# A two-block network on one core: the layer norms' mean from DVE's addition, routing reordered, constant products in PE's waits

## The chip, the core and the metric

The kernel is one program on one of the eight cores of a Trainium2 chip. The core's engines have instruction streams of their own and meet through semaphores: TensorE (PE, matrix products), VectorE (DVE), ScalarE (ACT), GpSimd (POOL) and SyncE (SP, which here issues the transfers from device memory). The metric is device microseconds for one execution. PE's clock has two levels, 1.2 and 2.4 GHz; the profile gives the granted clock of a stretch as a share of the higher one (PEclk).

## What is computed

The input is 256 tokens of 1024 features, f32. First block, two layers of this form (all f32, 2816 hidden columns in the feed-forward parts):

```
h = h + 0.5 * rmsnorm(swiglu(rmsnorm(h, g1), w_gate, w_up, w_down), g2)
h = h + rmsnorm(mixer(rmsnorm(h, g3)), g4)
h = h + 0.5 * rmsnorm(swiglu(rmsnorm(h, g5), w_gate, w_up, w_down), g6)

def mixer(u):                       # u @ w_in, split in z, xbc, dt, u5, g_a, g_b
    y_a = ssd_branch(z, xbc, dt) @ w_branch_a     # conv, silu, chunked state space, group norm
    y_b = s5_branch(u5) @ w_branch_b              # complex diagonal scan, gelu, glu
    return (sigmoid(g_a) * y_a + sigmoid(g_b) * y_b) @ w_out
```

Second block, two layers, `ALPHA = (2 * DEPTH) ** 0.25`:

```
layer 0: main = short convolution mixer;  ffn = swiglu (dense)
layer 1: main = causal attention of 12 heads with rotary positions;  ffn = 8 experts, 2 for each token
x = layer_norm(ALPHA * x + concat(main, memory_attention) @ w_o)
x = layer_norm(ALPHA * x + ffn)

def layer_norm(x, g, b):            # mean and variance over the 1024 features
    mu = mean(x);  var = mean((x - mu) ** 2)
    return (x - mu) * rsqrt(var + 1e-5) * g + b
```

## The kernel before

Every large product is made of three: weights and activations are each split into a high part (f32 rounded to the matrix format) and a low part, and hi x hi, lo x hi and hi x lo are added up in PSUM. A weight chunk is 128 x 2048 f32 (1.05 MB). SP loads it into one of three slots of `raw`; ACT rounds it into `w_hi` (`convert`, L1157) once PE has used the slot's last chunk; DVE subtracts (`w_lo`, L1594) and signals `weights_ready`; PE multiplies. Each engine's order is written out by hand, and all engines walk the same list of chunks. Loops on the chip run over the two layers of the first block (PE only), the steps of a feed-forward part (three chunks a step) and the experts.

PSUM has eight banks. Banks 0 to 3 hold the accumulated output of a part, by token or by feature; banks 4 to 7 take the columns of the current chunk, which ACT evicts.

Stage borders. When a part's output stands in PSUM, ACT squares and sums it, takes the root (L1169), DVE inverts it, scales and adds to `H` (L1640), and for the next part's norm the same is done with `H`; DVE writes `scaled` (a view of `G`, L1617). PE waits for `scaled_ready` in `turn_stream` (L674), transposes 16 tiles of 128x128 into banks 0 to 3, ACT makes `x_hi` out of each pair of tiles, DVE `x_lo`, and PE's first product (L612) follows. In the second block the border is `layer_norm`: DVE adds `ALPHA * H` and the part's output for each half of the tokens (L2067), ACT sums each half with a copy into a spare tile (L1425), DVE forms minus the mean (L2071, event `centered`), ACT squares with that bias and sums (L1173), root, inverse, and DVE writes `H` (L2077, `h_ready`), which PE turns (L674).

Inside the first block's mixer, the state-space branch ends with a norm over four groups of features: ACT squares a group (L1374, `group_sq`), PE sums over features with a matrix of ones (`sum_features`, L686, f32 products of 128x256), ACT takes the root (L1323), DVE inverts and stages (`k_hi`, `k_lo`), and PE multiplies with `w_branch_a`. The output projection (`token_chunk(C_OUT + i, i, 4)`, L665) waits for the merge of both branches on DVE (L1952).

Attention goes over pairs of heads: PE scores (L927), DVE maximum, ACT exponent and sum, DVE division (L2106), PE turns the probabilities (L936), ACT copies them, PE multiplies with the values (L947).

The experts. PE computes 16 logits columns (L1016), DVE picks the two best experts (`masks_ready`), PE counts ranks (`ranks`), DVE makes `slot_of` and the number of passes (`n_pass`, event `routed`; one pass if no expert has more than 128 tokens). In a pass DVE writes `pick` (L2220), PE gathers the expert's tokens out of `H` (L1036), ACT and DVE make `x_hi` and `x_lo` (`expert_inputs`, L1514 and L2244), and then 88 steps follow (8 experts, 11 steps): `front` and `back` (two halves of the contraction, L1059), the hidden tile's turn (L1073), and `down` (L1084 to L1086). The weights have a ring of three buffers for each of front, back and down, converted by ACT (`high`, L1526) and DVE (`low`, L2250). SP loads the first front and back early, and the rest after `routed`. Before, ACT and DVE convert `down` 0 ahead of `expert_inputs`:

```
            with n.loop(act, passes, "pass"):
                high("down", 0)
                expert_inputs()
                high("front", 1)
                silu()
```

Of the kernel before, what the change touches and what calls it, by code (L numbers as in the profile page):

```python
# [27 lines left out]
P = 128  # L28
T = 256
D = 1024  # L30
# [202 lines left out]
def build(nc, a, out):  # L233

    ctx = ExitStack()
    with ctx:
# [48 lines left out]
        def flat(tiles):  # L285
# [74 lines left out]
                 "gains_in prm_psum prm_ready setup_done h_ready squared rooted xf_ready xh_ready x_ready gain_in weighed scaled_ready turned logit_ready "  # L360
# [7 lines left out]
                 "picked gathered scattered scatter_turned scatter_ready hidden_ready hidden_turned kh_ready y_copied sum_added mean_sum "  # L368
# [235 lines left out]
        def _(pe):  # L604
# [4 lines left out]

            def product(dst, slot, hi, lo, w0, start):  # L610

                mm(dst, w_hi[:, slot, w0:w0 + P], hi, start=start, stop=False, skip_group_check=True)  # L612
                mm(dst, w_lo[:, slot, w0:w0 + P], hi, start=False, stop=False, skip_group_check=True)  # L613
                return mm(dst, w_hi[:, slot, w0:w0 + P], lo, start=False, stop=True, skip_group_check=True)  # L614
# [208 lines left out]
            def mixer():  # L823
# [17 lines left out]
                ssd_output(7)  # L841
                end_run()
# [20 lines left out]
                n.due("acc_read")  # L863
                zero_acc(4)
# [8 lines left out]
            with n.loop(pe, DEPTH, "layer"):  # L873
                pe.wait_ge(s["gains_in"], n.due("gains_in", 16 * 10))
                for i in range(2):
                    last = nc.tensor.transpose(PS[:, 7, 96 * i:96 * i + 96], prm_rows[0:96, i, :], cst("ident", 96, 0, 96))
                last.then_inc(s["prm_psum"], n.one("prm_psum"))
                pe.wait_ge(s["prm_ready"], n.due("prm_ready"))
                turn_stream(scaled, "scaled_ready")
                ffn(rows=True)  # L880
                turn_stream(scaled, "scaled_ready")
                mixer()
                turn_stream(scaled, "scaled_ready")
                ffn()
# [33 lines left out]
            def attention(heads):  # L918
# [34 lines left out]
                for p in range(pairs):  # L953
                    if p:
                        outputs(p - 1)
                    if p + 2 < pairs:
                        scores(p + 2)
                    turn(p)
# [21 lines left out]
            attention(heads_a)  # L980
            zero_acc()
            for i in range(4):
                token_chunk(B_WO1 + i, i)
            turn_stream(H, "h_ready")
            ffn()
            turn_stream(H, "h_ready")
# [17 lines left out]
            end_run(waiting=True)  # L1004
            swap(rope_at[10])
            pe.wait_ge(s["roped"], n.due("roped", 2))
            attention(heads_b)
            zero_acc()
            for i in range(4):
                token_chunk(B_WO2 + i, i)  # L1010
            turn_stream(H, "h_ready")
# [6 lines left out]
            last.then_inc(s["logits"], n.one("logits"))  # L1018
            pe.wait_ge(s["masks_ready"], n.due("masks_ready"))
# [6 lines left out]
            last.then_inc(s["ranks"], n.one("ranks"))  # L1026
            pe.wait_ge(s["routed"], n.due("routed"))
# [93 lines left out]
            with n.loop(pe, passes, "pass"):  # L1121
                pe.wait_ge(s["sum_added"], n.due("sum_added"))
                gather(turned=False)
                zero_sum()
                pe.wait_ge(s["x_ready"], n.due("x_ready", 2))
# [13 lines left out]
                turn_hidden(wait=True)  # L1139
                down()  # L1140
# [4 lines left out]
        def _(act):  # L1145
# [275 lines left out]
            def layer_norm(split=True, late=None):  # L1421
                near_root()
                for t in range(2):
                    act.wait_ge(s["xf_ready"], n.due("xf_ready"))
                    last = fn(unused_2[:, t, :], H[:, t, :], ACT.Copy, accum_out=sums[:, 0, t:t + 1])  # L1425
                last.then_inc(s["mean_sum"], n.one("mean_sum"))
                act.wait_ge(s["centered"], n.due("centered"))
                for t in range(2):
# [78 lines left out]
            fn(rsm[:, 5, :], rsm[:, 4, :], ACT.Exp).then_inc(s["route_exp"], n.one("route_exp"))  # L1507
            act.wait_ge(s["routed"], n.due("routed"))
# [48 lines left out]
            with n.loop(act, passes, "pass"):  # L1557
                high("down", 0)
                expert_inputs()
# [19 lines left out]
        def _(dve):  # L1579
# [484 lines left out]
            def layer_norm(src, split=True, late=None):  # L2064

                for t in range(2):
                    stt(H[:, t, :], H[:, t, :], ALPHA, src[:, t, :], MULT, ADD).then_inc(s["xf_ready"], n.one("xf_ready"))  # L2067
                dve.wait_ge(s["xf_ready"], n.last("xf_ready"))
                dve.wait_ge(s["gain_in"], n.due("gain_in", 32))
                dve.wait_ge(s["mean_sum"], n.due("mean_sum"))  # L2070
                then_on(ts(sums[:, 2, :], sums[:, 0, :], -1.0 / D, None, MULT), "centered")  # L2071
# [106 lines left out]

            def small(i):
# [12 lines left out]

            dve.wait_ge(s["logits"], n.due("logits"))
# [17 lines left out]
            v.memset(moe_sum[:, :, :], 0.0)  # L2211
# [5 lines left out]

            def gather_pick():
                for t in range(2):
                    ins = ts(pick[:, t, :], cst("iota", P, 0, P), cur[:, t:t + 1], None, EQ)  # L2220
                return ins

            def first_pick():

                then(v.tensor_copy(cur[:, 0:2, None], slot_of[:, :, 0:1]))
                gather_pick().then_inc(s["picked"], n.one("picked"))
# [70 lines left out]
            with n.loop(dve, passes, "pass"):  # L2297
                first_pick()
                low("down", 0)
                expert_inputs()  # L2300
# [22 lines left out]
                then(ts(slot_of, slot_of, -float(SLOTS), None, ADD))  # L2323
            layer_norm(moe_sum, split=False)
# [52 lines left out]
```

## Time and profile before

| what | value |
|---|---|
| median of 3 runs | 3215.32 us (3211.72 to 3215.64) |
| profiled execution | 3210.52 us |
| its span, first to last instruction | 3208.7 us |
| mean granted clock of PE | 0.955 |
| PE busy | 2953.6 us, 92% of the span |
| DVE busy | 2233.0 us, 70% |
| ACT busy | 1673.4 us, 52% |
| GpSimd busy | 74.2 us, 2% |
| read from device memory | 616.81 MB, 193 GB/s over the span |

The engines run side by side, so their shares don't add up to 100%. A busy PE is not always a fast one: where the granted clock is 0.5, the same product is busy for nearly twice as long. In a list of waits an engine's idle time stands beside the instruction that ended it and the one that released it.

### The profile page before, as it was taken

How to read it: one execution, taken by the hardware profiler on the slowest of the kernel's cores; microseconds unless marked ns; L12 is line 12 of the kernel's file. 1: busy time of each engine (PE TensorE's matmuls, PEld its weight loads, DVE VectorE, ACT ScalarE, POOL GpSimd, SP SyncE). 2: the span in 40 equal slices, each digit the busy share in tenths (PEclk: the TensorE clock that was granted, in tenths of full speed). 3: DMA queues.
4: the chain of work that ended last, by engine and by line, in shares of the span. 5: the costliest groups of instructions: out<-in, count | busy, mean ns of one | idle time of the engine just before them, and what ended most of it. 6: DMA issues, size and time to landing. Idle time of an engine off the chain costs nothing.

```text
span 3208.7 us, 51731 instructions
## 1 busy us (share of the span) xinstructions
PE 2953.6 (92%) x20597; PEld 2645.5 (82%) x20597; DVE 2233.0 (70%) x2614; ACT 1673.4 (52%) x1838; POOL 74.2 (2%) x68
## 2 busy tenths in 40 slices
PE   8988899989989988898989998998679999999997
PEld 7988898979989888888879896998467877787775
DVE  5778975655556779857555554555658888888887
ACT  4444566334444444563344443444446776677665
POOL 0000013000000000030000000000000000000000
PEclk9998999999999988999999998999879999999999
DMA  7553342446545533433545453555079999999995
GB/s 238 167 155 105 93 139 86 158 143 199 177 156 185 177 105 94 119 118 108 176 156 196 159 183 118 178 176 171 14 262 328 344 336 342 328 327 343 351 327 191
DMA packets 488733, 619.87 MB, mean 193 GB/s; under 512 B 34689, under 2 KB 439059, under 8 KB 488595
## 3 DMA queue, kind: packets, MB, share of 16 engines
q1 hardware_dynamic: 488595, 617.91, 58.3%
q8 instruction: 101, 1.65, 0.2%
q14 instruction: 37, 0.30, 0.0%
HBM read 616.81 MB, written 1.05 MB: 193 GB/s over the span
## 4 chain that ended last, share of the span: by engine, by line
PE 77%; DVE 14%; ACT 5%; issue 3%; DMA 0%; DVEq 0%; SPq 0%; ACTq 0%
PE PS L1059 13%; PE PS L612 12%; PE PS L613 12%; PE PS L614 12%; PE PS L665 12%; DVE w_lo L1594 3%; PE PS L1084 3%; PE PS L1086 3%; PE PS L1085 3%; ACT w_hi L1157 2%; ACT w_hi L1526 1%; PE PS L1094 1%; PE PS L794 1%; PE PS L1036 1%; PE PS L756 1%
## 5 line engine op out<-in xcount | busy, mean ns | idle before, releaser
L612 PE MATMUL PS<-x_hi,w_hi 128*128 128x256 f32 x3360 | 976.4, 291 | 11.5 <-DVE x_lo L2061 7.1
L613 PE MATMUL PS<-x_hi,w_lo 128*128 128x256 f32 x3360 | 966.8, 288 | 0.0
L614 PE MATMUL PS<-x_lo,w_hi 128*128 128x256 f32 x3360 | 965.5, 287 | 0.0
L1594 DVE TENSOR_TENSOR w_lo<-raw,w_hi 128x2048 fp32r<-128x2048 f32 x313 | 711.6, 2288 | 330.7 <-ACT w_hi L1157 330.0
L1157 ACT ACTIVATE w_hi<-raw 128x2048 fp32r<-128x2048 f32 x313 | 598.6, 1913 | 397.4 <-PE PS L665 248.0
L612 PEld LDWEIGHTS PS<-x_hi,w_hi 128*128 128x128 f32 x3360 | 662.1, 197 | 23.3 <-issue 12.0
L613 PEld LDWEIGHTS PS<-x_hi,w_lo 128*128 128x128 f32 x3360 | 662.4, 197 | 1.9
L614 PEld LDWEIGHTS PS<-x_lo,w_hi 128*128 128x128 f32 x3360 | 661.3, 197 | 0.0
L1059 PE MATMUL PS<-w_hi,x_hi 128*128 128x512 f32 x704 | 285.3, 405 | 9.5 <-DVE x_lo L2244 6.7
L1059 PE MATMUL PS<-w_lo,x_hi 128*128 128x512 f32 x704 | 276.7, 393 | 0.0
L1059 PE MATMUL PS<-w_hi,x_lo 128*128 128x512 f32 x704 | 275.3, 391 | 0.0
L2250 DVE TENSOR_TENSOR w_lo<-raw,w_hi 128x2048 fp32r<-128x2048 f32 x96 | 219.7, 2288 | 40.2 <-ACT w_hi L1526 39.8
L1659 DVE TENSOR_TENSOR k_hi<-act_out,PS 128x256 fp32r<-128x256 f32 x110 | 46.3, 420 | 279.4 <-PE PS L614 277.6
L2250 DVE TENSOR_TENSOR w_lo<-XC,w_hi 128x2048 fp32r<-128x2048 f32 x88 | 201.7, 2292 | 41.6 <-ACT w_hi L1526 41.4
L665 PE MATMUL PS<-w_hi,k_hi 128*128 128x512 f32 x568 | 179.9, 398 | 15.2 <-DVE k_lo L1952 13.6
L1526 ACT ACTIVATE w_hi<-raw 128x2048 fp32r<-128x2048 f32 x96 | 183.8, 1915 | 14.0 <-PE PS L1086 14.0
L665 PE MATMUL PS<-w_lo,k_hi 128*128 128x512 f32 x568 | 177.6, 394 | 0.0
L665 PE MATMUL PS<-w_hi,k_lo 128*128 128x512 f32 x568 | 177.1, 393 | 0.0
L1526 ACT ACTIVATE w_hi<-XC 128x2048 fp32r<-128x2048 f32 x88 | 168.3, 1912 | 8.3 <-PE PS L1059 8.3
L1211 ACT ACTIVATE act_out<-PS 128x256 f32<-128x256 f32 x55 | 21.1, 383 | 280.2 <-PE PS L614 280.2
L1059 PEld LDWEIGHTS PS<-w_hi,x_hi 128*128 128x128 f32 x704 | 132.9, 189 | 38.4 <-issue 10.9
L1059 PEld LDWEIGHTS PS<-w_lo,x_hi 128*128 128x128 f32 x704 | 132.7, 188 | 29.7
(401 smaller groups left out, 4491.7 us busy)
## 6 DMA issues: line engine op xcount, KB each, us to landing
XC<-in_w_gu_moe_dram SPq DMA_DIRECT2D x176, 512.0 KB, 8.8
raw<-in_w_gu_moe_dram SPq DMA_DIRECT2D x132, 512.0 KB, 7.9
raw<-in_w_in_dram SPq DMA_DIRECT2D x64, 1024.0 KB, 5.7
raw<-in_ffn_w_gate_dram SPq DMA_DIRECT2D x44, 1024.0 KB, 5.3
raw<-in_ffn_w_up_dram SPq DMA_DIRECT2D x44, 1024.0 KB, 6.8
raw<-in_ffn_w_down_dram SPq DMA_DIRECT2D x44, 1024.0 KB, 5.0
raw<-in_w_down_moe_dram SPq DMA_DIRECT2D x32, 1024.0 KB, 10.1
G<-in_w_down_moe_dram SPq DMA_DIRECT2D x32, 1024.0 KB, 9.5
```

The source lines that it names most:

```text
L612: mm(dst, w_hi[:, slot, w0:w0 + P], hi, start=start, stop=False, skip_group_check=True)
L613: mm(dst, w_lo[:, slot, w0:w0 + P], hi, start=False, stop=False, skip_group_check=True)
L614: return mm(dst, w_hi[:, slot, w0:w0 + P], lo, start=False, stop=True, skip_group_check=True)
L665: last = mm(PS[:, bank + 2 * t + b, :], left, right[:, slot, kt * D + 512 * b:kt * D + 512 * (b + 1)], start=False, stop=True, skip_group_ ...
L1059: last = mm(PS[:, 4, :], left, right, start=(k0 + k == 0 and right is whi and left is hi), stop=True, skip_group_check=True)
L1084: mm(PS[:, b, :], hi, whi, start=False, stop=True, skip_group_check=True)
L1085: mm(PS[:, b, :], lo, whi, start=False, stop=True, skip_group_check=True)
L1086: last = mm(PS[:, b, :], hi, wlo, start=False, stop=True, skip_group_check=True)
L1157: fn(w_hi[:, slot, :], raw[:, slot, :], ACT.Copy).then_inc(s["hi_ready"], n.one("hi_ready"))
L1526: fn(w_hi[:, MOE_SLOT[kind], :], MOE_RAW[kind][j % 3], ACT.Copy).then_inc(s["hi_ready"], n.one("hi_ready"))
L1594: tt(w_lo[:, slot, :], raw[:, slot, :], w_hi[:, slot, :].bitcast(F32), SUB)\
L2250: tt(w_lo[:, slot, :], MOE_RAW[kind][j % 3], w_hi[:, slot, :].bitcast(F32), SUB)\
```

## The change

It has these parts.

- `warm(bank, count)` on PE: `count` f32 products of the constant `ident` (128x128) with 256 columns of the constants, written into a bank that nobody reads. It is called at 13 places of the program text, 189 products in one execution; the four places in the loop over the first block's layers run twice, and the one in `attention` for both attentions, with 15 and 5.
- `layer_norm` (four calls): DVE's addition leaves its own sum (`accum_out`), DVE forms minus the mean of each half right behind it, and ACT's summing copies go. The events `xf_ready` and `mean_sum` go; ACT waits for `centered` once for each half.
- Routing: DVE zeroes `moe_sum` before it waits for the logits; `first_pick` is done before `n_pass` and, for a further pass, at the end of the pass; ACT calls Silu once on a column of `eps` before it waits for `routed`.
- In a pass, ACT and DVE do `expert_inputs` before `down` 0.

The diff, without the two lines of event names and the moved bodies of `gather_pick` and `first_pick`:

```diff
@@ PE
+            def warm(bank, count):
+
+                for _ in range(count):
+                    mm(PS[:, bank, 0:256], cst("ident"), con[:, 0:256], start=True, stop=True, skip_group_check=True)
...
                 ssd_output(7)
+                warm(0, 5)
                 end_run()
...
                 n.due("acc_read")
+                warm(6, 10)
                 zero_acc(4)
...
                 ffn(rows=True)
+                warm(4, 16)
                 turn_stream(scaled, "scaled_ready")
                 mixer()
+                warm(0, 16)
                 turn_stream(scaled, "scaled_ready")
                 ffn()
...
-            def attention(heads):
+            def attention(heads, wait):
...
                         scores(p + 2)
+                    if p == 0:
+                        warm(6, wait)
                     turn(p)
...
-            attention(heads_a)
+            attention(heads_a, 15)
             zero_acc()
             for i in range(4):
                 token_chunk(B_WO1 + i, i)
+            warm(4, 16)
             turn_stream(H, "h_ready")
             ffn()
+            warm(4, 16)
             turn_stream(H, "h_ready")
...
             end_run(waiting=True)
+            warm(0, 8)
             swap(rope_at[10])
             pe.wait_ge(s["roped"], n.due("roped", 2))
-            attention(heads_b)
+            attention(heads_b, 5)
             zero_acc()
             for i in range(4):
                 token_chunk(B_WO2 + i, i)
+            warm(4, 16)
             turn_stream(H, "h_ready")
...
             last.then_inc(s["logits"], n.one("logits"))
+            warm(6, 4)
             pe.wait_ge(s["masks_ready"], n.due("masks_ready"))
...
             last.then_inc(s["ranks"], n.one("ranks"))
+            warm(6, 3)
             pe.wait_ge(s["routed"], n.due("routed"))
...
                 zero_sum()
+                warm(6, 4)
                 pe.wait_ge(s["x_ready"], n.due("x_ready", 2))
...
                 turn_hidden(wait=True)
+                warm(3, 8)
                 down()
@@ ACT
                 for t in range(2):
-                    act.wait_ge(s["xf_ready"], n.due("xf_ready"))
-                    last = fn(unused_2[:, t, :], H[:, t, :], ACT.Copy, accum_out=sums[:, 0, t:t + 1])
-                last.then_inc(s["mean_sum"], n.one("mean_sum"))
-                act.wait_ge(s["centered"], n.due("centered"))
-                for t in range(2):
+                    act.wait_ge(s["centered"], n.due("centered"))
                     square_sum(H, t, "act_step", unused_2, bias=sums[:, 2, t:t + 1])
...
             fn(rsm[:, 5, :], rsm[:, 4, :], ACT.Exp).then_inc(s["route_exp"], n.one("route_exp"))
+            fn(eps[:, 4:5], eps[:, 0:1], ACT.Silu)
             act.wait_ge(s["routed"], n.due("routed"))
...
             with n.loop(act, passes, "pass"):
+                expert_inputs()
                 high("down", 0)
-                expert_inputs()
                 high("front", 1)
@@ DVE
                 for t in range(2):
-                    stt(H[:, t, :], H[:, t, :], ALPHA, src[:, t, :], MULT, ADD).then_inc(s["xf_ready"], n.one("xf_ready"))
-                dve.wait_ge(s["xf_ready"], n.last("xf_ready"))
+                    then(stt(H[:, t, :], H[:, t, :], ALPHA, src[:, t, :], MULT, ADD, accum_out=sums[:, 0, t:t + 1]))
+                    then_on(ts(sums[:, 2, t:t + 1], sums[:, 0, t:t + 1], -1.0 / D, None, MULT), "centered")
                 dve.wait_ge(s["gain_in"], n.due("gain_in", 32))
-                dve.wait_ge(s["mean_sum"], n.due("mean_sum"))
-                then_on(ts(sums[:, 2, :], sums[:, 0, :], -1.0 / D, None, MULT), "centered")
...
+            v.memset(moe_sum[:, :, :], 0.0)
             dve.wait_ge(s["logits"], n.due("logits"))
...
             then(ts(slot_of, slot_of, 1000.0, None, ADD))
-            v.memset(moe_sum[:, :, :], 0.0)
+            first_pick()
...
             with n.loop(dve, passes, "pass"):
-                first_pick()
+                expert_inputs()
                 low("down", 0)
-                expert_inputs()
                 low("front", 1)
...
                 then(ts(slot_of, slot_of, -float(SLOTS), None, ADD))
+                first_pick()
             layer_norm(moe_sum, split=False)
```

## Rows read from the trace of the kernel before

**Rows 1.** The page of the whole span, its first lines.
```profile
span 3208.7 us, 51731 instructions
...
PE 2953.6 (92%) x20597; PEld 2645.5 (82%) x20597; DVE 2233.0 (70%) x2614; ACT 1673.4 (52%) x1838; POOL 74.2 (2%) x68
```

**Rows 2.** The list of waits, PE alone: total us, times, longest us.
```profile
PE PS L674 <- DVE G L1617: 41.8, 6, 8.1
...
PE PS L674 <- DVE H L2077: 24.9, 3, 8.4
PE PS L665 <- DVE k_lo L1952: 13.6, 5, 5.5
PE PS L1084 <- DVE k_lo L2260: 13.2, 15, 4.5
...
PE PS L936 <- DVE work L2106: 11.2, 5, 8.0
```

**Rows 3.** Stretches: window, its us, busy us by engine, granted clock (PEclk), DMA.
```profile
218.00:221.40 3.40, 3.40 (x16) 3.27 (x16) 0.70 (x2) 0.97 (x3) 0.00 (x0) 0.50 0.00 0
221.50:224.90 3.40, 2.77 (x21) 2.64 (x21) 3.03 (x8) 3.40 (x7) 0.00 (x0) 1.00 0.00 0
567.00:570.40 3.40, 1.73 (x15) 1.71 (x15) 3.29 (x8) 1.91 (x1) 0.00 (x0) 1.00 0.72 292
1856.40:1859.80 3.40, 1.40 (x12) 1.20 (x10) 0.77 (x2) 1.96 (x5) 0.00 (x0) 1.00 0.82 286
```

**Rows 4.** The ten half-clock stretches behind waits that `warm` fills: two, and the sum.
```profile
682.30:689.00 6.70, 4.84 (x11) 3.80 (x12) 4.97 (x12) 0.00 (x0) 0.00 (x0) 0.50 0.56 181
...
1929.80:1945.10 15.30, 13.02 (x44) 7.87 (x45) 3.93 (x13) 3.14 (x6) 0.00 (x0) 0.50 0.00 0
...
sum 52.30, PE 47.90 PEld 38.73 DVE 25.89 ACT 18.89 POOL 0.00; mean PE 4.79 PEld 3.87 DVE 2.59 ACT 1.89 POOL 0.00
```

**Rows 5.** Timeline of PE: start us, us, instruction, count, idle before.
```profile
550.65 3.69 PE L686 MATMUL PS<-work,con 128*128 128x256 f32 x16 [1.21 <-ACT work L1374]
...
717.99 3.67 PE L674 MATMUL PS<-con,G 128*128 128x128 f32 x16 [8.07 <-DVE G L1617]
...
1823.33 1.91 PE L913 MATMUL PS<-con,XC 128*128 128x128 f32 x16
```

**Rows 6.** Timeline of ACT at the first group root.
```profile
547.80 1.28 ACT L1323 ACT_TABLE_LOAD   x1 [3.74 <-PE PS L686]
```

**Rows 7.** Timeline of DVE and ACT in the norm at 1965 us.
```profile
1965.44 2.35 DVE L2067 SCALAR_TENSOR_TENSOR H<-H,PS 128x1024 f32<-128x1024 f32 x2 [1.19 <-PE PS L665]
...
1972.32 2.48 DVE L2077 SCALAR_TENSOR_TENSOR H<-work,sums,conv_in 128x1024 f32<-128x1024 f32 x2
...
1970.37 0.19 ACT L1173 ACTIVATION_READ_ACCUMULATOR work<-H,sums 128x1 f32 x1
```

**Rows 8.** Timelines of PE, ACT and DVE from the logits to the experts.
```profile
2331.88 6.83 PE L1016 MATMUL PS<-prm,work 128*128 128x8 f32 x32
...
2349.28 6.43 PE L1036 MATMUL PS<-work,H 128*128 128x128 f32 x32 [5.44 <-DVE work L2220]
...
2362.97 0.79 PE L1059 MATMUL PS<-w_hi,x_hi 128*128 128x512 f32 x1 [6.73 <-DVE x_lo L2244]
...
2373.26 0.49 PE L1059 MATMUL PS<-w_hi,x_hi 128*128 128x512 f32 x1 [2.02 <-DVE stage L2256]
...
2356.11 1.28 ACT L1526 ACT_TABLE_LOAD   x1 [14.48 <-DMA raw<-in_w_down_moe_dram]
...
2344.83 1.76 DVE L2211 MEMSET U<- 128x2048 f32 x1 [0.49 <-DVE work L2210]
```

**Rows 9.** ACT's timeline, one expert step to the next; then a stretch.
```profile
2393.47 0.38 ACT L1535 ACTIVATE k_hi<-PS 128x256 fp32r<-128x256 f32 x1 [0.96 <-PE PS L1073]
...
2401.91 0.39 ACT L1535 ACTIVATE k_hi<-PS 128x256 fp32r<-128x256 f32 x1 [0.96 <-PE PS L1073]
...
2380.00:2390.00 10.00, 10.00 (x47) 8.24 (x46) 8.92 (x7) 7.89 (x6) 0.00 (x0) 1.00 1.08 364
```

More of the change, by code:

```diff
@@ L359, in build @@
         names = ("raw_a raw_b raw_c hi_ready weights_ready chunk_used consts_in x_in params_in params_done "
-                 "gains_in prm_psum prm_ready setup_done h_ready squared rooted xf_ready xh_ready x_ready gain_in weighed scaled_ready turned logit_ready "
+                 "gains_in prm_psum prm_ready setup_done h_ready squared rooted xh_ready x_ready gain_in weighed scaled_ready turned logit_ready "
                  "gate_a up_a silu_done staged c_evicted tap_done silu_conv c_ready c_psum b_ready in_psum in_ready cv_ready "
@@ L367, in build @@
                  "rope_ang rope_table rope_psum roped mixed logits gate_diff route_exp masks_ready ranks routed "
-                 "picked gathered scattered scatter_turned scatter_ready hidden_ready hidden_turned kh_ready y_copied sum_added mean_sum "
+                 "picked gathered scattered scatter_turned scatter_ready hidden_ready hidden_turned kh_ready y_copied sum_added "
                  "z_tanh moe_silu front_in_1 back_in_1 down_in_1 front_in_2 back_in_2 down_in_2 front_ready back_ready down_ready front_used back_used down_used "
@@ L2177, in _, with gather_pick, first_pick @@
             first = cst("first")[:, None, :].to_broadcast([P, 2, N_EXPERTS])
+            def gather_pick():
+                for t in range(2):
+                    ins = ts(pick[:, t, :], cst("iota", P, 0, P), cur[:, t:t + 1], None, EQ)
+                return ins
+            def first_pick():
+                then(v.tensor_copy(cur[:, 0:2, None], slot_of[:, :, 0:1]))
+                gather_pick().then_inc(s["picked"], n.one("picked"))
             def small(i):
@@ L2216, in _ @@
             passes = dve.value_load(n_pass[0:1, :].bitcast(I32), min_val=1, max_val=2)
[L2218 to L2226, printed above, removed]
             def make_picks(e, following=None):
```

## The prediction

> **What bounds the kernel now.** I read the page first: the one core's span is 3208.7 us, the profiled execution took 3210.52 us, and TensorE (PE) is busy 92% of the span [rows 1]. So a microsecond in which PE waits or runs slowly is, nearly everywhere, a microsecond of the end. Next I read the list of waits for PE alone [rows 2]: the long ones stand at the stage borders, where PE waits for VectorE (DVE) and ScalarE (ACT) to finish a norm (with `G` 41.8 us in six waits, of which five are about 8 us; with `H` three of 8.3 us), a softmax (8.0 us), the merge before the output projection (5.5 us, twice) and the last hidden tile (4.5 us). Then the granted clock. In the stretches view the reader sees that a wait costs twice: behind the border at 210 us PEclk is 0.50 (1.2 GHz against 2.4 GHz), and it is 1.00 again only after a stretch in which PE was busy throughout [rows 3]. The waits that the change fills are followed by ten such stretches with real work in them, 47.9 us of PE busy time at half clock [rows 4].
>
> **The price of a filling product.** `warm` issues plain f32 products of 128x256 with a 128x128 constant. The nearest rows are the group sums, the same shape and type: 16 records (two for each product) in 3.69 us at full clock, the last one's tail included, so 0.44 us a product [rows 5]. Sixteen take 7.0 us, 15 take 6.6, 10 take 4.4, 8 take 3.5. They start while the clock is still full. Against the waits of 8.07, 8.0, 5.5 and 4.5 us they leave 1.0 to 1.4 us idle, so they delay nothing there. Whether so short an idle piece drops the clock: a stretch at 567 us in which PE was busy 1.73 of 3.4 us has full clock all through and no fall behind it; the one at 1856 us, busy 1.40, was followed by a fall [rows 3]. The filled borders are busier than either, so I take it that the clock holds.
>
> **Stage borders in the first block (four of 16 products).** The transposes behind the wait take 3.67 us at half clock and 1.91 at full [rows 5]. ACT can start after ten of the 16, so the first product comes 1.0 us earlier, not 1.8. The first products then run at half clock for some 4 us at three borders (three of the ten stretches of [rows 4]); PE would do them in about half, but in the first tile it is fed by DVE one piece at a time, so I count 1.7, 1.2 and 1.7. At the fourth (210 us) the clock is back before them [rows 3]. Sum 4 x 1.0 + 4.6 = 8.6 us earlier. A rule weighs against this: by the Trainium skill, TensorE: Matmul & The Clock Gate, Part 4 (PE-mode transpose), transposes don't count as PE activity for the clock. This case's trace disagrees: from 218.0 to 221.4 us PE did nothing but the 16 transposes, and the clock came back right behind them [rows 3]. By the rule, the idle piece, the transposes and the wait behind them would be one pause, which is a rival below.
>
> **Output projection (10 products, twice).** The wait stays 5.5 us, the products behind it run at full clock: the 4.84 us busy at 682 us [rows 4] would take 0.53 of that, and a little more is gained at the second. Gain 2.3 + 2.6 = 4.9.
>
> **Group sums (5 products, twice).** Here PE has no wait to fill: the squares are ready, and ACT's first root waits 3.74 us for PE's sum [rows 6]. So 5 x 0.44 = 2.2 us go straight onto the path, through root, reciprocal and staging. Loss 4.4.
>
> **Attention.** In the first one (15 products in 8.0 us) 15.3 us of half clock follow, 13.0 busy [rows 4]; two turns, two outputs, the zeroing and the first projection would save up to 6.0, but PE pauses between them for ACT's copies, so that the clock is uncertain: I take 4.0 (1.5 to 6). In the second, 8 products (3.5 us) cover the wait for the last rotations, but PE pauses again right behind it, and 5 more (2.2 us) stand in front of a turn that is nearly ready: 1.0 (-1 to 3), an estimate.
>
> **Layer norms.** Before: DVE adds both halves (2.35 us), ACT sums both, then come DVE's negative mean, ACT's squares and root, and DVE's shift (2.48 for both) [rows 7]; PE waits 8.3 us for it [rows 2]. ACT's two summing passes go; DVE's addition leaves the sum. The new chain is DVE's: 1.2 (first half) + 0.3 + 1.2 + 0.3 + 2.45 (two centred halves) + 0.25 + 1.25 = 7.0 us. ACT's squares end before it. Gain 1.2 at each of four. The trace has no DVE addition with a sum; bounds: nothing more, or 0.2 a half, as ACT's read of its accumulator takes [rows 7] (gain 0.8). I take nothing more. By the Trainium skill, Vector Engine (DVE) Microarchitecture Reference, section 7, an operation of this kind with two f32 sources in SBUF runs at half throughput for want of a port for the accumulator. Only the last norm has both in SBUF; no row shows the case, and by the rule that norm would lose about 2 us instead of gaining 1.2. In the first two norms the 16 products (7.0 us) fill the new wait exactly. Transposes and first products add 0.9 and 0.8: 2 x 2.9 = 5.8 earlier.
>
> **Routing and the start of the experts.** From the third norm on: 1.2 (norm); 0.8 (transposes); the 32 logit records take 6.83 us at half clock [rows 8], 3.4 at full, and I take 2.5 of that (0 to 3.3); counts 0.6 (-0.7 to 1.1); on DVE the 1.76 us memset leaves the path and some 0.4 of `first_pick` is added that `routed` waits for, 1.4. Sum 6.5. From `routed` (2347.0 us, the memset's end and three small operations behind it) to the second front product PE needed 26.3 us (2373.26): gather 6.43 us at half clock, then 6.73 us of waiting because ACT converted `down` first, and that waited 14.48 us for its transfer [rows 8]. After the change the gather starts 1.6 us behind `routed` and takes 3.9; `expert_inputs` follows at once, x_lo is ready 1.5 to 2.8 later while four filling products run to 7.9. Front and back take 5.5 at full clock. But ACT converts `down` before the second front: it lands 9.1 behind `routed`, front 12.0 (one transfer of 1.05 MB takes 2.9 us at 364 GB/s), 1.9 for ACT, 2.3 for DVE, 0.4 for hidden: 16.7. Gain 9.6. Together 16.1 (8 to 19). One more row matters: a step's weights are 3.15 MB, 8.6 us at 364 GB/s, a step takes PE 8.4 [rows 9]; the lead shrinks by 0.2 a step for nine steps and just lasts. The table load for Silu goes before the loop; whether another stays is 1.3 us at most, inside the bounds.
>
> **End.** Eight products keep the clock for the last `down`: 1.7. The norm: 1.2. `first_pick` now stands at the end of the pass: loss 0.7. Sum 2.2.
>
> **Sum:** -8.6 - 4.9 + 4.4 - 4.0 - 1.0 - 5.8 - 16.1 - 2.2 = -38.2. The profiled execution would take 3172.3 us. It lies 4.8 below the median of 3215.32, and I carry the difference over to that: 3177. The waits inside the mixers aren't touched; their half-clock pieces depend on where a pause falls and can move the sum by 3.
>
> **Rivals.** (a) The clock falls again behind the transposes (the two idle pieces added together, as at 1856 us [rows 3]): half clock for the first products at seven borders, 1.7 each as counted above, 12 back: 3189. For it: a border keeps 1.0 idle in front of the transposes and about as much behind. Against: the transposes restored the clock at 218 us [rows 3]. (b) The experts become bound by transfers: the order is right, the weights don't land. DMA already runs at 364 GB/s [rows 9], with nothing in reserve for the earlier start, so up to 9.6 comes back: 3187. (c) The change doesn't do what it says: constant products don't hold the clock. Then only the norms, the memset and the new order count, less the group sums: about -5.5, 3210. (d) Slower: the products themselves run at half clock. At the transposes' ratio (3.67 to 1.91) one costs 0.85 us, 16 cost 13.5 in front of every border: 5.5 more at four, 5.3 at three, 3 at two projections, 4.7 and 5 in the attentions, 2.3 at the end, 8.5 at the sums, less 6.5: +58, 3273. It decides from 0.50 us a product (8.07 / 16); the price of 0.44 has little room. Against it, the group sums ran at full clock.
>
> **How the numbers follow.** Forecast 0.62, (a) 0.15, (b) 0.12, (c) 0.05, (d) 0.03; 0.03 for more than I count. About 0.2% (6.4 us) is what a measurement of this kernel can tell. Forecast, (a), (b) and the surplus are faster: 0.92; (c) is no change: 0.05; slower 0.03. The forecast's own range comes from the bounds above, 3163 to 3188; to hold 8 in 10 the range takes in (a) and (b) with their spread: 3162 to 3197.
>
> **What would show it.** At each border PEclk 1.00, transposes in 1.9 us, 16 products of 0.44; H's transposes 7.0 us behind the last product; the group sums 2.2 us later; the second front product about 17 us after `routed`, and PE without waits for `w_lo` in the first expert. It would be wrong if PEclk is 0.50 behind the filling products, if a DVE addition with sum takes more than 1.5 us, or if PE waits for weights in the first expert.

## The result, and the profile after

The changed kernel takes 3178.61 us (median of four runs, 3174.41 to 3183.69) against 3213.52 us (four runs, 3210.54 to 3215.64): a ratio of 0.9895, 95% interval 0.9876 to 0.9913, or 34.9 us less. The forecast was 3177, from 38.2 us less and a median before of 3215.32. The profiled execution took 3183.69 us, its span is 3181.7 us, 27.0 below the span of [rows 1]; it is one of the two longer of the four. The mean granted clock of TensorE rose from 0.955 to 0.974.

The page, its first lines:

```profile
span 3181.7 us, 52486 instructions
...
PE 3007.6 (95%) x20975; PEld 2690.0 (85%) x20975; DVE 2235.2 (70%) x2629; ACT 1664.3 (52%) x1822; POOL 74.2 (2%) x68
```

PE is 54 us busier than in [rows 1] although the span is shorter. The 189 constant products are 378 more instructions and some 83 us of work that nobody reads. A busier engine is not a better one here; what counts is the clock at which the useful products run.

The list of waits, PE alone (total us, times, longest us):

```profile
PE PS L752 <- DVE work L1841: 33.0, 15, 4.8
PE PS L679 <- DVE G L1633: 14.5, 6, 8.1
...
PE PS L1101 <- DVE k_lo L2275: 9.8, 15, 1.1
...
PE PS L670 <- DVE k_lo L1968: 5.4, 6, 1.2
PE PS L945 <- DVE work L2120: 4.5, 5, 1.3
...
PE PS L679 <- DVE H L2091: 0.2, 1, 0.2
```

Against [rows 2], with `G` 41.8 us became 14.5, with `H` 24.9 became 0.2, and the longest in front of the output projection fell from 5.5 to 1.2. One wait of 8.1 us with `G` is still there: the turn into the second layer of the first block, which `warm` does not fill. The largest item of the list stands inside the mixers and is untouched.

Stretches (window, us, busy us by engine with counts, granted clock, DMA share, GB/s):

```profile
218.00:221.50 3.50, 2.02 (x17) 1.73 (x16) 1.64 (x4) 1.11 (x4) 0.00 (x0) 1.00 0.00 0
221.50:225.00 3.50, 2.63 (x20) 2.60 (x21) 3.17 (x8) 3.50 (x7) 0.00 (x0) 1.00 0.00 0
688.60:692.01 3.41, 3.41 (x8) 2.69 (x9) 3.14 (x8) 0.00 (x0) 0.00 (x0) 0.50 0.76 233
917.29:930.94 13.65, 8.76 (x40) 8.36 (x40) 8.40 (x14) 8.92 (x16) 0.00 (x0) 0.50 0.62 192
2330.41:2337.24 6.83, 5.96 (x25) 5.16 (x24) 0.95 (x6) 0.00 (x0) 0.00 (x0) 0.50 0.68 164
2350.00:2360.00 10.00, 10.00 (x47) 8.19 (x46) 7.05 (x6) 6.30 (x5) 0.00 (x0) 1.00 1.09 366
```

The first two lines answer to the first two of [rows 3]: the border at 210 us, 1.2 us idle in front of the transposes and 1.2 behind them, now has full clock in both. The next three are stretches where the clock is at half although a filled wait lies in front, or, at 917 us, because none was filled. The last one is the experts' first step.

PE's timeline:

```profile
547.26 3.09 PE L613 MATMUL PS<-con 128*128 128x256 f32 x10
...
688.52 1.18 PE L670 MATMUL PS<-w_hi,k_hi 128*128 128x512 f32 x2 [1.22 <-DVE k_lo L1968]
...
2312.47 7.07 PE L613 MATMUL PS<-con 128*128 128x256 f32 x32
2319.63 2.29 PE L679 MATMUL PS<-con,H 128*128 128x128 f32 x16
2321.95 3.74 PE L1031 MATMUL PS<-prm,work 128*128 128x8 f32 x32
...
2329.66 2.19 PE L613 MATMUL PS<-con 128*128 128x256 f32 x6
2332.71 5.98 PE L1053 MATMUL PS<-work,H 128*128 128x128 f32 x32 [0.87 <-DVEq L2241]
...
2348.71 0.49 PE L1076 MATMUL PS<-w_hi,x_hi 128*128 128x512 f32 x1 [2.08 <-DVE stage L2271]
```

At 2312.47 the reader sees the price of the filling: 16 products, 32 records, in 7.07 us, against 7.0 in the prediction. That is the price at full clock. The five products at 547.26 took 3.09 us and the three at 2329.66 took 2.19, 0.6 to 0.7 each, since the clock was at half for a part of both (PEclk 0.77 and 0.67 over them). The transposes behind the 16 start at once and take 2.29 us, the logits 3.74 in place of 6.83 [rows 8]. The second front product is at 2348.71 in place of 2373.26.

DVE's timeline in the norm at 1962 us, at the end of the routing, and in the last norm; then ACT's in the first group sum and in the first expert:

```profile
1961.79 1.22 DVE L2083 SCALAR_TENSOR_TENSOR H<-H,PS 128x1024 f32<-128x1024 f32 x1 [1.14 <-PE PS L670]
1962.94 0.08 DVE L2083 DVE_READ_ACCUMULATOR H<-H,PS 128x1 f32 x1
1963.06 0.15 DVE L2084 TENSOR_SCALAR sums<-sums 128x1 f32<-128x1 f32 x1
...
1967.41 2.48 DVE L2091 SCALAR_TENSOR_TENSOR H<-work,sums,conv_in 128x1024 f32<-128x1024 f32 x2
...
2331.31 0.15 DVE L2240 CAST work<-work 128x1 int32<-128x1 f32 x1
...
3170.42 1.22 DVE L2083 SCALAR_TENSOR_TENSOR H<-H,U 128x1024 f32<-128x1024 f32 x1
...
552.16 1.28 ACT L1342 ACT_TABLE_LOAD   x1 [6.56 <-PE PS L691]
...
2340.81 1.92 ACT L1542 ACTIVATE w_hi<-raw 128x2048 fp32r<-128x2048 f32 x1 [1.00 <-DMA raw<-in_w_down_moe_dram]
```

From the addition's start to the end of the first half of `H` the norm takes 6.9 us (1961.79 to 1967.41 and 1.24 more), where the prediction had 7.0. ACT's root at the group sum now waits 6.56 us for PE, 3.74 before [rows 6]. In the experts ACT waits 1.00 us for `down`, 14.48 before [rows 8], and needs no table load in front of it.

**Where the time went.** I subtract the start of the same product in the two traces, place by place. First-block borders -1.1, -2.8, -2.5 and -2.9; output projections -0.7 and -1.0; group sums +2.8 and +2.2; first attention -2.6; second attention +1.7; the first two norms with their transposes and first products -2.8 and -2.8; third norm, routing and the first expert up to the second front product -17.0; the last `down` -1.6, the rest of the end -0.8. What remains, +5, lies where the change has nothing, in half-clock pieces that fell otherwise: the start of the kernel (+1.2), the two mixers (+1.4 and +2.5), the unfilled turn into the second layer (+2.0), and the entry into the second block (-2.2). Together -27.0.

### The profile page after: what moved, and what is told of

Its sections match the earlier page's. It is cut to its first block, busy times and chain, and to the rows that moved or that the text cites. A ratio compares the mean times of both kernels' runs of the same rounds, so it can differ in the third digit from the quotient of the medians.

```text
span 3181.7 us, 52486 instructions
## 1 busy us (share of the span) xinstructions
PE 3007.6 (95%) x20975; PEld 2690.0 (85%) x20975; DVE 2235.2 (70%) x2629; ACT 1664.3 (52%) x1822; POOL 74.2 (2%) x68
## 4 chain that ended last, share of the span: by engine, by line
PE 78%; DVE 14%; ACT 5%; issue 3%; DVEq 0%; DMA 0%; SPq 0%; ACTq 0%
PE PS L1076 13%; PE PS L617 12%; PE PS L618 12%; PE PS L619 12%; PE PS L670 12%; DVE w_lo L1610 3%; PE PS L1101 3%; PE PS L1103 3%; PE PS L1102 3%; ACT w_hi L1176 2%; PE PS L1053 1%; ACT w_hi L1542 1%; PE PS L1111 1%; PE PS L761 1%; PE PS L799 1%
## 5 line engine op out<-in xcount | busy, mean ns | idle before, releaser
L617 PE MATMUL PS<-x_hi,w_hi 128*128 128x256 f32 x3360 | 972.4, 289 | 15.6 <-DVE x_lo L2077 8.4
L617 PEld LDWEIGHTS PS<-x_hi,w_hi 128*128 128x128 f32 x3360 | 657.7, 196 | 26.3 <-issue 13.3
```

## The experiments

Each is compared with the kernel before on the same chip; "spans" are those of the profiled runs. All of them compute the whole reference.

**The products alone.** The kernel before with `warm` and its calls, nothing else:

```diff
+            def warm(bank, count):
+                for _ in range(count):
+                    mm(PS[:, bank, 0:256], cst("ident"), con[:, 0:256], start=True, stop=True, skip_group_check=True)
...
+                warm(0, 5)
...
+                warm(4, 16)
                 turn_stream(scaled, "scaled_ready")
```

> The kernel before with all 189 constant products on PE and nothing else of the change. Theory (the products hold PE's clock through the long waits): about 24 us below before, 3189 us, the stage borders at PEclk 1.00 and the transposes behind them in about 2 us; the wait for the second block's norms stays at 8.3 us. Rival (the gain is that of the shorter chains and the new order, the products hold nothing): at or above before, 3213 to 3220, since 2.2 us of products stand on the path twice.

Measured 3189.34 us (3186.53 to 3192.23), ratio 0.9925 (0.9908 to 0.9941), 23.8 us less, clock 0.974 as in the changed kernel. Rival (c), that constant products don't hold the clock, and rival (d), that they run at half clock, are out.

**Everything but the products.** The changed kernel, `warm` issues nothing:

```diff
-                for _ in range(count):
+                for _ in range(0):
```

> The changed kernel with warm() issuing nothing: the norms, the routing and the new order alone. Theory: about 10 us below before, 3203, because the norms give 1.2 each and the expert phase starts some 6 us earlier, with the gather and the first expert products at half clock. Rival (products hold nothing and only cost): at or below the changed kernel, 3178 or less.

Measured 3198.00 us (3195.61 to 3200.13), ratio 0.9955 (0.9938 to 0.9971), 15.2 us less, clock 0.957. That is 5 us better than I expected. In the trace next to nothing moves up to the first norm; then -1.9 and -1.3 at two norms and -12.0 up to the first expert product. PE's and DVE's timeline there:

```profile
2338.99 6.44 PE L1053 MATMUL PS<-work,H 128*128 128x128 f32 x32 [2.91 <-DVEq L2241]
...
2356.92 0.49 PE L1076 MATMUL PS<-w_hi,x_hi 128*128 128x512 f32 x1 [2.04 <-DVE stage L2271]
...
2337.59 0.15 DVE L2240 CAST work<-work 128x1 int32<-128x1 f32 x1
```

From `routed` (the end of the cast, 2337.74) to the second front product it takes 19.2 us, in the changed kernel 2348.71 - 2331.46 = 17.25, before 26.3. So 7.1 of the 9.1 us that this distance lost come without any filling. I had credited the rest of the stage too much to the clock.

**The norms alone.** The kernel before with the new `layer_norm` on both engines:

```diff
-                    stt(H[:, t, :], H[:, t, :], ALPHA, src[:, t, :], MULT, ADD).then_inc(s["xf_ready"], n.one("xf_ready"))
+                    then(stt(H[:, t, :], H[:, t, :], ALPHA, src[:, t, :], MULT, ADD, accum_out=sums[:, 0, t:t + 1]))
+                    then_on(ts(sums[:, 2, t:t + 1], sums[:, 0, t:t + 1], -1.0 / D, None, MULT), "centered")
```

> The kernel before with the layer norms' part alone (the mean from DVE's addition). Theory (DVE's chain bounds each norm, 1.2 us less each): 4.9 us below before, 3208, in the trace H's first transpose 7.1 us behind the last product instead of 8.3. Rival (the addition with a sum runs at half rate, at least where both sources lie in SBUF): no gain, and the last norm about 2 us longer.

Measured 3204.27 us (3202.41 to 3204.49), ratio 0.9971 (0.9960 to 0.9982), 8.6 us less where 4.9 was the sum. Each wait for `H` is 1.25 us shorter (7.00 for 8.25), as counted. Norms two and four gave -1.3 each. The first gave -2.1, since the half-clock stretch at it was 6.8 us long in place of 10.2. The third gave -4.0 up to the first expert product. PE's timeline there:

```profile
2325.91 3.67 PE L674 MATMUL PS<-con,H 128*128 128x128 f32 x16 [7.00 <-DVE H L2071]
2329.38 3.73 PE L1016 MATMUL PS<-prm,work 128*128 128x8 f32 x32
```

The wait is 7.00 us, and the logits behind it ran at full clock (3.73 us against 6.83 [rows 8]), without one filling product. The extra 3 us are the clock's, and they came from a wait that was only 1.25 us shorter. It repeats: the run without products has the same wait of 7.00 us and the same 3.73 us of logits, while the two runs below that keep the old norm (order alone, routing alone) have 8.25 and 6.83, as before. That it would come I could not foretell from the trace before.

**The order alone.** The kernel before with the experts' inputs ahead of `down`, on ACT and on DVE:

```diff
+                expert_inputs()
                 high("down", 0)
-                expert_inputs()
```

> The kernel before with only the order changed: expert_inputs ahead of down 0 on ACT and DVE. Theory (ACT sat behind the transfer of the first down while the gathered tokens were ready): first expert product some 4.5 us earlier and the second front product as much, 3208.5. Rival (the transfers are what the experts wait for): the first product earlier, the second front product not, and the end where it was, 3213.

Measured 3209.17 us (3204.43 to 3211.18), ratio 0.9986 (0.9977 to 0.9995), 3.7 us less. Timelines of PE and DVE:

```profile
2360.43 0.49 PE L1059 MATMUL PS<-w_hi,x_hi 128*128 128x512 f32 x1 [1.55 <-DVE x_lo L2244]
...
2369.84 0.49 PE L1059 MATMUL PS<-w_hi,x_hi 128*128 128x512 f32 x1 [2.07 <-DVE stage L2256]
...
2349.46 0.15 DVE L2215 CAST work<-work 128x1 int32<-128x1 f32 x1
```

From `routed` (2349.61) the second front product is 20.2 us away, 26.3 before: 6.1 less. PE waits 1.55 us for `x_lo`, 6.73 before [rows 8]. This run reached the routing 2.6 us late by half-clock pieces elsewhere, which is why the total shows only part of it.

**The routing alone.** The kernel before with the zeroing of `moe_sum` ahead of the logits, `first_pick` ahead of `routed`, and the Silu table loaded ahead of the loop:

```diff
+            v.memset(moe_sum[:, :, :], 0.0)
             dve.wait_ge(s["logits"], n.due("logits"))
...
-            v.memset(moe_sum[:, :, :], 0.0)
+            first_pick()
...
+            fn(eps[:, 4:5], eps[:, 0:1], ACT.Silu)
             act.wait_ge(s["routed"], n.due("routed"))
```

> The kernel before with the routing part alone: the zeroing of moe_sum ahead of the logits, the first pick ahead of routed, Silu's table loaded ahead of the loop; no products, no new norms, the old order of down and the expert inputs. Theory (additive): what the run without products gained, 15.0 in its trace, less the norms (8.2 at their own places) and the order (4.5): 2.3 faster, 3211; from the norm to routed 1.4 less, the gather 1.5 sooner behind it, but the first expert product still waits for down to land and be converted. Rival (the parts need one another): 7 us faster, 3206, or nothing at all, because the transfer of down is the last to come either way.

Measured 3208.40 us (3206.87 to 3213.16), ratio 0.9988 (0.9978 to 0.9997), 4.6 us less. Timelines of PE and ACT:

```profile
2363.04 0.79 PE L1059 MATMUL PS<-w_hi,x_hi 128*128 128x512 f32 x1 [6.78 <-DVE x_lo L2246]
...
2357.47 1.91 ACT L1527 ACTIVATE w_hi<-raw 128x2048 fp32r<-128x2048 f32 x1 [11.36 <-DMA raw<-in_w_down_moe_dram]
```

That is 2 us more than I expected. The gather now comes 2.5 us early, but ACT still waits 11.36 us for `down` and PE as long as before (6.78 against 6.73). What the part gives is that `routed` comes sooner, since `down` lands 9 us behind `routed` whatever stands in front. The three medians, 8.6 + 3.7 + 4.6 = 16.9, make the 15.2 of the run without products: the parts add up within what these runs can tell, and need nothing of one another. With the products' 23.8 on top it would be 39.0; the change gives 34.9, so some 4 us are bought twice: the third norm's logits, for one, get full clock by either.

**No products at the group sums.**

```diff
-                warm(0, 5)
                 end_run()
```

> The changed kernel without the five products in front of the group sums (twice). Theory (no wait is filled there, they lie on the path): 4.4 us faster than the changed kernel, 3174, with the first product of the branch projection 2.2 us earlier behind the last state-space output. Rival (they keep the clock for what follows and pay for themselves): no faster, with a half-clock stretch in the group sums or the first products behind them.

Measured 3176.11 us (3171.16 to 3181.24), ratio 0.9888 (0.9870 to 0.9905). In the traces the first product behind each sum comes 2.3 and 2.2 us sooner, counted from the last product before the sum. The medians show 2.5 of the 4.5, and the runs of either kernel spread by 9 to 10 us. In the traces these ten products only cost.

**Longer filling, 24 for 16, at the seven borders.**

```diff
-                warm(4, 16)
+                warm(4, 24)
```

> The changed kernel with 24 instead of 16 products at the seven stage borders, three of them norms of the second block. Theory (0.44 us a product, in order, 1.0 us spare at the first block's borders and none at the second's): 8 more cost 3.5 us, so 2.5 us at four borders and 3.4 at three, 20 us slower than the changed kernel, about 3199. Rival (the products run beside the wait or at another price): under 5 us slower, or 40 and more if they run at half clock.

Measured 3196.00 us (3193.61 to 3203.13), ratio 0.9954 (0.9937 to 0.9970), 17.4 more than the changed kernel. PE's timeline at the first border:

```profile
209.49 10.52 PE L613 MATMUL PS<-con 128*128 128x256 f32 x48
219.85 1.91 PE L679 MATMUL PS<-con,G 128*128 128x128 f32 x16
```

24 products take 10.52 us, 0.438 each. The block's borders come 2.1 us late each (10.5 - 8.07 = 2.4 is the most that it could be), the norms' 2.7 to 2.8 (10.5 - 7.0 = 3.5). Together 17 us: the price holds, and what reaches past the wait is paid for.

**Shorter filling, 8 for 16, at the same seven.**

```diff
-                warm(4, 16)
+                warm(4, 8)
```

> The changed kernel with 8 in place of 16 filling products at the seven borders (four in the two block layers, three norms of the following part): 3.5 us of work and then 4.6 us (3.5 at the norms) without. Theory (a wait that is half filled still drops the clock): each border loses again what the filling gave, the transposes take 3.67 in place of 1.91 us and the first products run at half clock, but no border gets longer: 7 x 2.0 = 14, less about 1 for scatter: 3191. Rival (it is enough to break the pause in two): the clock stays, the time stays 3178.6, and half the products were for nothing.

Measured 3194.43 us (3192.72 to 3195.35), ratio 0.9943 (0.9927 to 0.9960), 15.8 more than the changed kernel. A wait that is half filled drops the clock. The first border, stretches and then PE's timeline:

```profile
218.00:221.50 3.50, 3.14 (x15) 3.14 (x16) 0.97 (x2) 0.70 (x2) 0.00 (x0) 0.50 0.00 0
221.50:225.00 3.50, 2.94 (x14) 2.54 (x13) 3.22 (x8) 3.50 (x8) 0.00 (x0) 0.50 0.00 0
```

```profile
210.12 3.62 PE L613 MATMUL PS<-con 128*128 128x256 f32 x16
218.36 3.68 PE L679 MATMUL PS<-con,G 128*128 128x128 f32 x16 [4.62 <-DVE G L1633]
```

With 4.62 us idle behind 3.62 us of filling, the transposes take 3.68 us, and the first products behind them are at half clock too. The rival, that it is enough to break the pause in two, is out: 8 products are too few for these waits, and 24 too many. Lengths between were not run.

**No products in the second attention.**

```diff
-            warm(0, 8)
             swap(rope_at[10])
...
-            attention(heads_b, 5)
+            attention(heads_b, 0)
```

> The changed kernel without the 8 and the 5 products around the start of the second attention. Theory after the result (5 products stood in front of a turn that was ready, and the clock fell in the pause between them anyway): 1.5 us faster than the changed kernel in that stretch, PEclk 0.50 there as in the kernel before. Rival (they are worth the 1.0 us that the prediction gave them): 1.0 us slower there.

Measured 3178.47 us (3170.73 to 3186.29), ratio 0.9889 (0.9868 to 0.9909): no difference in the median where I expected 1.5, and a spread of 15.6 us that would hide it. PE's timeline without them, then with them:

```profile
2250.14 1.75 PE L945 MATMUL PS<-con,work 128*128 128x128 f32 x8
2253.01 1.08 PE L956 MATMUL PS<-work,XC 128*64 128x256 f32 x8 [1.11 <-ACT work L1465]
```

```profile
2249.68 3.50 PE L613 MATMUL PS<-con 128*128 128x256 f32 x10
2253.02 1.04 PE L945 MATMUL PS<-con,work 128*128 128x128 f32 x8
2255.17 1.08 PE L956 MATMUL PS<-work,XC 128*64 128x256 f32 x8 [1.11 <-ACT work L1466]
```

The five products stand where nothing is awaited, and the first output is at 2255.17 in place of 2253.01; 0.4 of these 2.2 us lay there before the attention began. So without all thirteen the first output and the first projection behind the attention come 1.8 us sooner. The other eight do hold the clock while they run (1.00 against 0.50 from 2234.6 to 2241.6 us), but PE waits there anyway, and the clock falls behind them: the scores gain some 0.7 us by it, and the five products cost 2.5.

**More waits filled.** The changed kernel without the sums' products, with ten at each layer's last turn (the 8.1 us wait that was left), products ahead of each long wait for `cv_ready` inside the mixers, and seven ahead of the third scores of the second attention in place of five in front of its turn:

```diff
             def s5_in(t):
+                warm(3, {0: 5, 1: 6, 4: 2, 5: 2, 6: 2, 7: 9}.get(t, 0))
                 pe.wait_ge(s["cv_ready"], n.due("cv_ready"))
...
-                warm(0, 5)
...
                 ffn()
+                warm(4, 10)
...
+                    if p == 0 and pairs > 2:
+                        warm(6, wait)
                     if p + 2 < pairs:
                         scores(p + 2)
-                    if p == 0:
+                    if p == 0 and pairs == 2:
                         warm(6, wait)
...
-            attention(heads_b, 5)
+            attention(heads_b, 7)
```

> A version meant to beat both: the changed kernel without the products ahead of the group sums; in the second attention 7 products in the pause before the third scores instead of 5 before the first turn; 2 to 9 products in the mixers' waits for cv_ready (s5_in, tiles 0, 1, 4 to 7), and 10 at the end of each layer's last feed-forward part. Theory (each wait filled with no more than its length keeps the clock at full): 4.4 us from the group sums, 2 from the attention, 1 to 2 at the layer's end, and 8 to 12 from the mixers, where 40 us of each layer run at half clock: about 3162. Rival (in the mixers PE waits for DVE anyway, so a faster PE only waits longer): 3171, the mixers' length unchanged though PEclk is 1.00.

Measured 3153.23 us (3148.21 to 3157.03), ratio 0.9821 (0.9807 to 0.9834): 59.6 us below the kernel before and 25.4 below the changed one. It is the fastest of the study, 9 us below what I expected. Stretches view, 520 us that hold the first feed-forward part and most of the first mixer, of this kernel and then of the changed one:

```profile
20.00:540.00 520.00, 497.17 (x4532) 464.11 (x4530) 398.05 (x581) 271.84 (x387) 36.97 (x32) 0.98 0.45 141
```

```profile
20.00:540.00 520.00, 492.00 (x4461) 462.80 (x4462) 391.64 (x571) 266.09 (x373) 31.38 (x28) 0.95 0.44 139
```

**The same without the mixers' products.**

```diff
             def s5_in(t):
-                warm(3, {0: 5, 1: 6, 4: 2, 5: 2, 6: 2, 7: 9}.get(t, 0))
                 pe.wait_ge(s["cv_ready"], n.due("cv_ready"))
```

> The kernel with more waits filled (3153.2 us) without the products inside the mixers: the changed kernel less the five products before each group sum, with ten products at the end of each block layer's last feed-forward part and seven products ahead of the third scores of both attentions' kind. Theory (the mixers' own pauses drop the clock and cost most of what the products there give back): against the changed kernel about 5 us less for the sums, 1.5 to 3 for the layer's start, 1 to 2 for the second attention: 3170, and against the kernel with more waits filled 15 to 18 us more, all of it inside the two mixers. Rival (the layer's start is what matters, the clock at the start carries through the mixer): within 4 us of 3153.

Measured 3173.51 us (3169.98 to 3175.32), ratio 0.9881 (0.9865 to 0.9898). So 20.3 of the 25.4 us are the mixers' waits, which are 0.6 to 4.8 us long in the changed kernel, and the other 5.1 are the sums, the layer's turn and the second attention together, which no run tells apart. In the traces the two mixers are 7.7 and 10.2 us shorter. I had expected 8 to 12 us from the mixers; why it was twice that is open.

## Why the prediction came out right, step by step

**The price of a product.** 0.44 us, worked out from the group sums [rows 5]; 7.07 / 16 = 0.44 in the changed kernel, 10.52 / 24 = 0.438 in the longer filling. Where the clock had fallen before, it was 0.6 to 0.7.

**First-block borders, -8.6.** Measured -9.3. Full clock before and behind, as in the stretches above. On the transposes, the Trainium skill (TensorE: Matmul & The Clock Gate, Part 4, PE-mode transpose) says that full clock does not engage for them, since they do not count as PE-busy in the same way. The changed kernel can't decide it, as the clock never fell there. With the short filling it was still 0.50 in the 3.5 us behind the transposes, where in [rows 3] it was 1.00. And among the five kernels whose code at this border fills nothing, the clock came back right behind the transposes in three (before, without products, order alone), while it stayed at 0.50 for 4.6 us and more behind them in two (norms alone, 222.2 to 226.8 us, and routing alone). So the row by which I contradicted the rule repeats in some kernels only, and the question is open. What was right is the consequence: 1.2 us idle, transposes and 1.2 us idle again lose nothing.

**Output projection, -4.9.** Measured -1.7: mis-sized. The wait is filled (1.22 us left of 5.5), but at both places PE's clock still fell a little later, 688.60 to 692.01 above, now for real products. A wait filled is not a clock held; the sum took all 4.84 us of half-clock work down to 0.53 of it and made no allowance for a later fall.

**Group sums, +4.4.** Measured +5.0, and +4.5 by the run without them. Rightly counted as pure loss.

**First attention, -4.0.** Measured -2.6, inside its 1.5 to 6: the clock fell behind the products for two short stretches, as was allowed for.

**Second attention, -1.0.** Measured +1.7: the wrong sign, and outside my bounds, a gain of -1 to 3. The step that failed is "5 more stand in front of a turn that is nearly ready", which I priced below the gain of the clock; the run without them shows 2.5 us on the path for the five and some 0.7 gained by the eight.

**First two norms, -5.8.** Measured -5.7. DVE's addition with the sum takes 1.22 us a half, 0.08 for the read of the accumulator and 0.15 for the mean, where I had 1.2 and 0.3. By the Trainium skill (Vector Engine (DVE) Microarchitecture Reference, section 7) the last norm, both sources in SBUF, should have run at half throughput. It takes the same 1.22 us (3170.42) as with a source in PSUM (1961.79): the trace disagrees, and the last norm gained 1.26 us (from the addition's start to the end of `H` 9.36 us before, 8.10 now). The "about 2 us" that I had that norm lose by the rule was also wrongly added up: twice 1.2 more on 8.10 makes 10.5, a loss of 1.1.

**Routing and the start of the experts, -16.1.** Measured -17.0. The second front product is 17.25 us behind `routed` where the working gave 16.7; the weights' landing sets it, and ACT's wait for `down` is 1.00. Two parts erred against each other: the gather ran at half clock for most of its length (5.98 us for 3.9; 2330.41 to 2337.24 above), and the logits gained all 3.1 us, not 2.5. Rival (b), that the experts become bound by transfers, is out: PE is busy 10.00 of 10.00 us at 366 GB/s, and the lead over the kernel before is 24.6 us both at the second front product and at the last `down`.

**End, -2.2.** Measured -2.4.

**What the sum did not have.** +5 in parts that the change does not touch. The prediction gave the mixers' half-clock pieces 3 us of scatter and named no term for the wait of 8.1 us that stays unfilled at 913 us; behind it the clock was at half for 13.65 us where it had been for 6.8. Together with the projection (3.2 short), the attentions (4.1 short), the sums (0.6) and a surplus of 1.7 in the others, this takes the profile to -27.0 from -38.2. The medians differ by 34.9, because the profile before was 3.0 us below its median and the one after 5.1 above: two runs of the changed kernel took 3183, two others 3174.5, and no trace shows why. The nearness of 3177 to 3178.61 is partly luck: this scatter is in it, and I started from a median of 3215.32 where the later one is 3213.52, which hid 1.8 of the 3.3 us by which the gain was overrated. The mechanism and the large terms are shown, the last 5 us are not.

Rival (a), the clock falling again behind the transposes at seven borders, did not happen at the borders; it did in small at the projections and attentions, where PE pauses several times in a row. Rival (c) was priced too low: the parts other than the products gave 15.2 us without any filling, so less the group sums it would have been some 11 us and not 5.5.

## What to carry to other kernels

Where one engine is the bound and its clock depends on its being busy, look for its waits in order of length and price them twice, once as the wait and once as the slow stretch behind; fill a wait to within about a microsecond of its end (what 16 products did here), not half (15.8 us lost) and not beyond (17.4 us lost). Fill only where a wait is: a product in front of work that is ready costs its full 0.44 us, as at the group sums and in the second attention. The short waits in a row, 0.6 to 4.8 us inside the mixers, were worth 20 us, nearly as much as all 189 products of the change (23.8).

## What the runs showed of the hardware that I had not expected

- The half-clock stretch behind one and the same wait varies: at 913 us it was 13.65 us long behind 8.1 us of waiting in the changed kernel, 6.8 us behind 7.7 in the kernel before. Runs of one kernel spread by 2.1 us (norms alone) to 15.6 us (no products in the second attention); each kernel has one trace, so the cause is open.
- The same code differs from trace to trace by more than most parts of the change are worth: from the third border to the fourth, where both do the same, the kernel with the short filling took 9.1 us less than the changed kernel. A difference of a few microseconds between two profiles has to be found at its place to mean anything.
- A shortening of one wait by 1.25 us, from 8.25 to 7.00, brought 3.1 us of clock with it at the third norm when nothing was filled, 0.8 at the first norm and none at the second, the same in both traces that have it (norms alone, and without products).
- With the short filling PE was busy nearly throughout from the third norm's transposes on (19.3 of 20.5 us), and the clock stayed at half all that while; this stage was the largest step of that run (3.8 us at the first expert product, 7.8 shortly behind the second front product). Why it did not rise sooner is open.
- DVE's read of its accumulator takes 0.08 us, ACT's 0.19 [rows 7].
